# Sums of squares and decay sums in two rounded passes in a two-block transformer kernel

## What is computed

```
q = rms_norm(q, sb_q_norm_w); k = rms_norm(k, sb_k_norm_w)      # stick-breaking branch
z = q @ k.T * scale                                             # by blocks of 128 rows
log_1mb = where(causal, log_sigmoid(-z), 0)
suffix = cumsum(log_1mb, reverse) - log_1mb
a = where(causal, exp(log_sigmoid(z) + suffix), 0);  o_sb = a @ v
...
qkv = silu(causal_depthwise_conv(gdn_qkv, gdn_conv_w))          # gated delta rule branch
gq = l2_normalize(gq); gk = l2_normalize(gk)                    # x * rsqrt(sum(x*x) + eps)
g = -exp(a_log) * softplus(gdn_a + dt_bias)
gc = cumsum(g);  decay = exp(gc_i - gc_j) for j <= i
T = inverse(eye + strictly_lower(k_beta @ k.T * decay))         # per chunk
o_gdn = chunked recurrence over states with T, decay, exp(gc)
```

## Time and profile before

| | us |
|---|---|
| median of 3 runs | 2774.71 |
| runs | 2766.96 to 2775.35 |
| profiled execution | 2777.7 |
| its span | 2776.0 |
| TensorE busy in it | 2666.2 (96%) |
| DVE, ACT, POOL busy | 1846.9, 1200.8, 527.0 |
| TensorE in the chain that ended last | 82% of the span |
| mean granted TensorE clock | 0.985 of full speed |

### The profile page before, as it was taken

How to read it: one execution, slowest core, us unless ns; L and a number is a source line. 1 busy time by engine, 2 the same in 40 slices (tenths; PEclk the granted TensorE clock), 3 DMA queues, 4 the chain that set the end, 5 groups by cost and what they waited for, 6 DMA issues and landing times.

```text
span 2776.0 us, 36053 instructions
## 1 busy us (share of the span) xinstructions
PE 2666.2 (96%) x13669; PEld 2289.8 (82%) x13669; DVE 1846.9 (67%) x3462; ACT 1200.8 (43%) x1941; POOL 527.0 (19%) x410
## 2 busy tenths in 40 slices
PE   8999999999998999999998999999999999999997
PEld 6887888887777999998997888888888656788886
DVE  4445665655665788876985888888987494544434
ACT  5554445343223444447994333333332454423222
POOL 0111111010001778772000111111110033000000
PEclk9999999999999999999999999999999999999999
DMA  4112110005662587865668898898986211222220
GB/s 168 54 54 83 70 46 31 31 31 212 210 213 104 215 299 279 280 230 203 256 245 297 331 346 336 331 350 321 344 336 219 82 57 49 97 91 91 97 101 31
DMA packets 141212, 501.14 MB, mean 181 GB/s; under 512 B 13256, under 2 KB 66928, under 8 KB 111472
## 3 DMA queue, kind: packets, MB, share of 16 engines
q1 hardware_dynamic: 122608, 364.60, 36.9%
q0 software_dynamic: 18432, 134.23, 12.2%
HBM read 450.53 MB, written 48.25 MB: 180 GB/s over the span
## 4 chain that ended last, share of the span: by engine, by line
PE 82%; DVE 8%; ACT 4%; DMA 3%; issue 1%; POOL 1%; SPq 0%; ACTq 0%; DVEq 0%; POOLq 0%
PE bank L250 22%; PE bank L252 22%; PE bank L251 22%; PE bank L2175 2%; DVE xn L1552 2%; DMA w_raw<-in_w_in_dram 2%; PE bank L1130 2%; PE bank L1146 1%; PE bank L2658 1%; DVE whl L246 1%; PE bank L748 1%; ACT whl L240 1%; PE bank L1136 1%; PE bank L2765 1%; PE bank L2692 1%
## 5 line engine op out<-in xcount | busy, mean ns | idle before, releaser
L250 PE MATMUL bank<-HH,uhl 128*128 128x384 f32 x1024 | 346.4, 338 | 1.9 <-POOL uhl L1678 1.9
L252 PE MATMUL bank<-HH,uhl 128*128 128x384 f32 x1024 | 343.5, 335 | 0.0
L251 PE MATMUL bank<-HL,uhl 128*128 128x384 f32 x1024 | 343.3, 335 | 0.0
L250 PE MATMUL bank<-vhl,awhl 128*128 128x512 f32 x768 | 301.6, 393 | 10.7 <-DVE awhl L2392 9.7
L251 PE MATMUL bank<-vhl,awhl 128*128 128x512 f32 x768 | 301.2, 392 | 0.0
L252 PE MATMUL bank<-vhl,awhl 128*128 128x512 f32 x768 | 300.7, 392 | 0.0
L1734 POOL DMA_INDIRECT gs<-in_uv_dram,idx x128 | 153.1, 1196 | 771.3 <-DVE x L1759 489.0
L2332 ACT ACTIVATE vhl<-vraw 128x1024 fp32r<-128x1024 f32 x128 | 135.7, 1061 | 324.3 <-PE bank L252 274.9
L1678 POOL TENSOR_TENSOR uhl<-ur,uhl 128x1024 fp32r<-128x1024 f32 x69 | 168.1, 2448 | 321.4 <-ACT uhl L1672 321.2
L246 DVE TENSOR_TENSOR whl<-w_raw,whl 128x2048 fp32r<-128x2048 f32 x49 | 113.9, 2325 | 168.5 <-ACT whl L240 168.5
L250 PE MATMUL bank<-HH,whl 128*128 128x512 f32 x528 | 213.9, 405 | 4.6 <-DVE whl L246 4.1
(11 more groups left out here) (434 smaller groups left out, 6105.6 us busy)
## 6 DMA issues: line engine op xcount, KB each, us to landing
ur<-in_peer_u_dram SPq DMA_DIRECT2D x128, 512.0 KB
vraw<-in_peer_v_dram SPq DMA_DIRECT2D x128, 512.0 KB
w_raw<-in_w_in_dram SPq DMA_DIRECT2D x36, 1024.0 KB, 4.9
xn<-in_ada_rows_dram SPq DMA_DIRECT2D x48, 512.0 KB, 4.7
g_scratch<-stg SPq DMA_DIRECT2D x12, 2048.0 KB, 8.2
gti<-g_scratch SPq DMA_DIRECT2D x16, 1536.0 KB, 12.3
wf_raw<-in_f_w_in_dram SPq DMA_DIRECT2D x22, 1024.0 KB, 4.8
act_scratch<-ag SPq DMA_DIRECT2D x96, 192.0 KB
```

What stands on the lines that cost most here:

```text
L250: e.matmul(out, l[0], r[0], start=start, stop=False)
L251: e.matmul(out, l[0], r[1], start=False, stop=False)
L252: return e.matmul(out, l[1], r[0], start=False, stop=stop)
```

## The change

Four edits, all in the mixer of the first block.

1. The matmuls with ones over squares, in both branches, become two fp32r passes: over the squares rounded, and over the rest. In the stick-breaking branch ACT rounds (into `eg_r`) right after the square, DVE subtracts (into `DT_r`), and the root of the tile before now follows these on ACT instead of leading. The very first sum moves behind the third projection. In group 0 of the delta rule DVE does both steps, for all four tiles, after its last weight split of the stage. In groups 1 to 3 ACT rounds the query squares in step 11, DVE subtracts in steps 12 and 13; the key squares move from step 16 to 14 and from the tile `cin` to the tile X of the inverse, DVE rounds and subtracts in step 15, their sums and roots move from step 18 to 16 and their normalisation from 20 to 18, while that of the query tiles goes from 15 to 20.
2. The decay sums become two fp32r passes over the high and low part of g (`ggr`), which DVE splits once.
3. For pair 3, ACT makes the high part of the logarithms, in step 2 ahead of the decays, and DVE only the low part, in step 2 ahead of the convolution; before DVE did both in step 3.
4. The new tiles lie over the same memory as fp32 tiles that are free at that time.

```diff
--- before.py
+++ after.py
@@ -452,17 +452,29 @@
...
+    ggr = new.sb("ggr", [P, 2, NT, 8], F32R)
...
+    DT_r = [new.sb(f"DT_r{i}", [P, S], F32R) for i in range(2)]
+    PM_r = [new.sb(f"PM_r{i}", [P, S], F32R) for i in range(2)]
+    eg_r = new.sb("eg_r", [P, 2, S], F32R)
...
-    squares_of = lambda g: ([cin[i % 2][:, 3:] for i in range(4)] if g else
-                            [zs[i // 2][:, (i % 2) * S:(i % 2 + 1) * S] for i in range(4)])
+    half_z = lambda x, i: x[i // 2][:, (i % 2) * S:(i % 2 + 1) * S]
+    squares_of = lambda g: ([cin[i][:, 3:] for i in range(2)] + [flat(HB[f]["X"]) for f in range(2)] if g else
+                            [half_z(zs, i) for i in range(4)])
+    sq_high = lambda g: ([x[:, :] for x in DT_r + PM_r] if g else [half_z(Llo, i) for i in range(4)])
+    sq_low = lambda g: ([x[:, 3:] for x in cin_r] + [flat(HB[f]["X_r"]) for f in range(2)] if g else
+                        [half_z(zs_r, i) for i in range(4)])
@@ -483,8 +495,9 @@
...
-        e.wait_ge(*A.of("sq", g, i))
-        e.matmul(b[:, :], ones, squares_of(g)[i], start=True, stop=True).then_inc(*T.up("gn", g, i))
+        e.wait_ge(*V.of("sq_lo", g, i))
+        e.matmul(b[:, :], exact("ones"), sq_high(g)[i], start=True, stop=False)
+        e.matmul(b[:, :], exact("ones"), sq_low(g)[i], start=False, stop=True).then_inc(*T.up("gn", g, i))
...
     def act_gdn_proj(e, R, g, i):
@@ -499,7 +512,7 @@
...
             elif g:
-                e.wait_ge(*V.of("gq", g - 1, 2 + i))
+                e.wait_ge(*V.of("gq", g - 1, i))
@@ -516,9 +529,28 @@
...
+        elif i < 2:
+            e.wait_ge(*V.of("cv", g, 4 + i))
...
-            e.wait_ge(*(V.of("gq", g, i - 2) if i >= 2 else V.of("cv", g, 4 + i)))
+            e.wait_ge(*GH[0].of("xt", 2 * g - 4 + i, LV - 1))
...
+    def act_gdn_high(e, g, i):
+        T, A, V, G = GP
+        e.wait_ge(*GH[2].of("vT", 2 * g - 2 + i))
+        e.wait_ge(*A.of("sq", g, i))
+        e.activation(sq_high(g)[i], squares_of(g)[i], ACT.Copy).then_inc(*A.up("sq_hi", g, i))
...
+    def dve_gdn_high(e, g, i):
+        T, A, V, G = GP
+        e.wait_ge(*A.of("sq", g, i))
+        e.tensor_copy(sq_high(g)[i], squares_of(g)[i]).then_inc(*V.up("sq_hi", g, i))
...
+    def dve_gdn_sqlow(e, g, i):
+        T, A, V, G = GP
+        e.wait_ge(*(A if g and i < 2 else V).of("sq_hi", g, i))
+        e.tensor_tensor(sq_low(g)[i], squares_of(g)[i], r32(sq_high(g)[i]),
+                        ALU.subtract).then_inc(*V.up("sq_lo", g, i))
...
     def act_gdn_root(e, R, g, i):
@@ -571,9 +603,12 @@
...
+        if h < 2:
+            e.wait_ge(*SB[2].of("g_lo"))
...
-            i = e.matmul(b[:, blk(tb)], gg[:, tb, h:h + 1].broadcast_to([P, P]), const("triu"), start=True,
-                         stop=True)
+            for part in range(2):
+                i = e.matmul(b[:, blk(tb)], ggr[:, part, tb, h:h + 1].broadcast_to([P, P]), exact("triu"),
+                             start=part == 0, stop=part == 1)
...
     def act_decay(e, R, h):
@@ -640,8 +677,9 @@
...
-        e.wait_ge(*A.of("sq", pair, wi))
-        e.matmul(b[:, :], ones, scr[wi % 2], start=True, stop=True).then_inc(*T.up("nrm", pair, wi))
+        e.wait_ge(*V.of("sq_lo", pair, wi))
+        e.matmul(b[:, :], exact("ones"), eg_r[:, wi % 2, :], start=True, stop=False)
+        e.matmul(b[:, :], exact("ones"), DT_r[wi % 2][:, :], start=False, stop=True).then_inc(*T.up("nrm", pair, wi))
...
     def act_sb_norm(e, pair, wi):
@@ -673,6 +711,8 @@
...
+            if (pair, seg) == (0, 2):
+                pe_sb_norm(e, 0, 0)
@@ -695,8 +735,6 @@
         if seg in (0, 2, 4):
...
         if seg < 4:
-            if seg:
-                act_sb_norm(e, pair, seg - 1)
@@ -705,6 +743,10 @@
...
+            e.wait_ge(*A.of("sq", pair, seg))
+            e.activation(eg_r[:, seg % 2, :], scr[seg % 2], ACT.Copy).then_inc(*A.up("sq_hi", pair, seg))
+            if seg:
+                act_sb_norm(e, pair, seg - 1)
@@ -718,6 +760,10 @@
     def dve_sb_proj(e, pair, seg):
         if seg in (0, 2, 4):
...
+        if seg < 4:
+            e.wait_ge(*SB[1].of("sq_hi", pair, seg))
+            e.tensor_tensor(DT_r[seg % 2][:, :], scr[seg % 2], r32(eg_r[:, seg % 2, :]),
+                            ALU.subtract).then_inc(*SB[2].up("sq_lo", pair, seg))
@@ -798,7 +844,7 @@
...
-        if seg == 3:
+        if seg == 3 and pair < 3:
@@ -809,6 +855,16 @@
...
+    def act_sb_high(e, hh):
+        T, A, V, G = SB
+        e.wait_ge(*G.of("L", 3, hh, NT - 1))
+        e.activation(Lhi[hh][:, :], Ls[hh][:, :], ACT.Copy).then_inc(*A.up("hi", 3, hh))
...
+    def dve_sb_low(e, hh):
+        T, A, V, G = SB
+        e.wait_ge(*A.of("hi", 3, hh))
+        e.tensor_tensor(Llo[hh][:, :], Ls[hh][:, :], r32(Lhi[hh][:, :]), ALU.subtract).then_inc(*V.up("lo", 3, hh))
...
     def dve_sb_sum(e, pair, hh):
@@ -856,7 +912,7 @@
...
-            e.matmul(b[:, 0:32], const("triu"), flat(gg), start=True, stop=True).then_inc(*T.up("gc"))
+            e.matmul(b[:, 0:32], r32(exact("triu")), flat(gg), start=True, stop=True).then_inc(*T.up("gc"))
...
     def act_ba(e, seg):
@@ -907,6 +963,10 @@
...
+            e.wait_ge(*V.of("g"))
+            e.tensor_copy(ggr[:, 0, :, :], gg[:, :, :]).then_inc(*V.up("g_hi"))
+            e.wait_ge(*V.of("g_hi"))
+            e.tensor_tensor(ggr[:, 1, :, :], gg[:, :, :], r32(ggr[:, 0, :, :]), ALU.subtract).then_inc(*V.up("g_lo"))
         if seg == 5:
@@ -929,7 +989,6 @@
...
-        pe_sb_norm(e, 0, 0)
@@ -990,6 +1049,7 @@
...
                         if seg == 2:
+                            act_sb_high(e, h)
...
                         if seg == 3:
@@ -1004,7 +1064,7 @@
...
-        e.tensor_copy(cst_r[:, i:i + 2, :], cst[:, i:i + 2, :]).then_inc(*SB[2].up("exact"))
+        e.tensor_copy(cst_r[:, i:i + 3, :], cst[:, i:i + 3, :]).then_inc(*SB[2].up("exact"))
@@ -1020,12 +1080,18 @@
...
+                    if seg == 2:
+                        dve_sb_low(e, 0)
+                        dve_sb_low(e, 1)
...
                         if seg == 2:
...
                         if seg == 3:
...
+        for i in (2, 3, 0, 1):
+            dve_gdn_high(e, 0, i)
+            dve_gdn_sqlow(e, 0, i)
@@ -1069,8 +1135,12 @@
...
+        X_r = [new.sb(f"X_r{i}", [P, NT, P], F32R) for i in range(2)]
...
+        for i in range(2):
+            HB[i].update({"X": X[i], "X_r": X_r[i]})
@@ -1320,8 +1390,9 @@
...
-                    if g < 3 and seg in (14, 18):
-                        pe_gdn_ones(e, R3, g + 1, (2 if seg == 18 else 0) + f)
+                    if g < 3 and seg in (14, 16):
+                        pe_gdn_ones(e, R3, g + 1, seg - 14 + f)
+                for f in range(2):
@@ -1349,12 +1420,14 @@
                     if seg == 11:
...
+                            act_gdn_high(e, g + 1, i)
...
+                    if seg == 14:
+                        for i in (2, 3):
+                            act_gdn_square(e, g + 1, i)
...
-                        if seg in (14, 18):
-                            act_gdn_root(e, R3, g + 1, (2 if seg == 18 else 0) + f)
-                        if seg == 16:
-                            act_gdn_square(e, g + 1, 2 + f)
+                        if seg in (14, 16):
+                            act_gdn_root(e, R3, g + 1, seg - 14 + f)
                         if seg == 17:
...
                         if seg == 19:
@@ -1378,9 +1451,15 @@
...
                     if seg in STEP:
...
+                    if seg in (12, 13):
+                        dve_gdn_sqlow(e, g + 1, seg - 12)
...
-                        if seg in (15, 20):
-                            dve_gdn_normed(e, g + 1, (2 if seg == 20 else 0) + f)
+                        if seg == 15:
+                            dve_gdn_high(e, g + 1, 2 + f)
+                            dve_gdn_sqlow(e, g + 1, 2 + f)
+                        if seg in (18, 20):
+                            dve_gdn_normed(e, g + 1, (2 if seg == 18 else 0) + f)
+                    for f in range(2):
                         if seg == 18:
...
                         if seg == 22:

```

More of the change, by code:

```diff
@@ L454, in build @@
     gg = new.sb("gg", [P, NT, 8])
[L455 to L459 removed]
+    ggr = new.sb("ggr", [P, 2, NT, 8], F32R)
+    new.sb("after_ggr", [P, 64])
+    with ExitStack() as ph:
+        cin = [new.sb(f"cin{i}", [P, S + 3], scope=ph) for i in range(2)]
+    cin_r = [new.sb(f"cin_r{i}", [P, S + 3], F32R) for i in range(2)]
+    qkv = [[new.sb(f"gq{i}", [P, S]) for i in range(8)]]
+    with ExitStack() as ph:
+        DTs = [new.sb(f"DTs{i}", [P, NT, P], scope=ph) for i in range(2)]
+        PMs = [new.sb(f"PMs{i}", [P, NT, P], scope=ph) for i in range(2)]
+        eg2 = new.sb("eg2", [P, 2, NT, P], scope=ph)
+    DT_r = [new.sb(f"DT_r{i}", [P, S], F32R) for i in range(2)]
+    PM_r = [new.sb(f"PM_r{i}", [P, S], F32R) for i in range(2)]
+    eg_r = new.sb("eg_r", [P, 2, S], F32R)
     EGs = [eg2[:, i, :, :] for i in range(2)]
@@ L622, in build @@
```

(12 more changed lines are left out.)

4 lines of the change are left out of this document (removed).

## The result

| | before | after |
|---|---|---|
| median, us | 2773.40 | 2783.46 |
| runs, us | 2766.96 to 2775.35 (6) | 2780.39 to 2787.76 (6) |
| profiled execution, its span | 2777.7, 2776.0 | 2784.2, 2782.4 |

The changed kernel is 10 us slower, ratio 1.0044 (95% interval 1.0030 to 1.0059). It lies in the range of the forecast (2763 to 2787) and just inside the likeliest case's own (2770 to 2784), but on the side to which the prediction gave 17 in 100: slower by over 0.3%. The forecast was +2.2 us.

The account below looks back on a forecast made before the run. TensorE, busy 96% of the span, was taken to bound the kernel, with in-order queues feeding it. Stage terms summed to -0.6 us, plus 2.8 for clock falls, on the median 2774.7: 2777 us, range 2763 to 2787.

Parts of the forecast that it names:

- the clock: TensorE's clock falling behind new waits: two of them cost 1.4 us each, +2.8 us.
- Two passes for one matmul: Sums of squares over 512 columns: 0.86 us becomes 0.46, saving 0.40 us in each of 32, 12.8 if all kept.
- rival 3: Two fp32r passes with "ones" cost as much as the fp32 matmul: 2781 us; chance 0.03.
- Blocks of pairs 1 and 2: Stick-breaking blocks: waits of 0.6 and 2.1 us behind DVE's queue, +1.1 us per block, +2.2 for two.
- Pair 3: Last logarithms: the 5.1 us wait becomes 0.4, bank waits of 2.0 and 2.4 come; projection and output 3.6 us earlier.
- First squares: First delta rule sums: TensorE waits 3.1 us behind DVE's weight split, key products start 2.8 us later.
- Groups: Delta rule groups 1 to 3: new waits outweigh savings, +0.5 us per group, +1.5 in all.
- Start: Start to pair 0: first sum's 0.8 us wait goes, four sums save 1.6, third subtraction 0.5 late; net -1.9 us.
- In the block in which pair 0's heads run: Stick-breaking block with pair 0's heads: ACT has 5.5 us more per step, nothing is late, -1.6 us.
- Decays: Decay sums in two passes of 128 columns: 0.4 us saved per two heads, four times; bounds 0 to 0.9.
- rival 2: Each new wait drops the clock: ten falls of 1.4 us give +13, 2788 us; decides from seven; chance 0.14.
- Rival 1: ACT and DVE chains are not late, overlooked slack hides the new steps: -22.9 us, 2752; chance 0.2.

Follow-up runs that it names:

- the first squares' reordering: The changed kernel with group 0's four casts and subtractions ahead of DVE's last weight split: 2776.80 us, ratio 1.0019 to the kernel before.
- where it was run alone: The kernel before with only pair 3's logarithms split by ACT and the decay sums in two passes: 2771.39 us, ratio 0.9998.
- +3.1 alone: The kernel before with only group 0's four delta rule sums of squares in two passes: 2776.03 us, ratio 1.0014.
- the sums were run alone: The kernel before with only the stick-breaking sums of squares in two passes: 2775.64 us, ratio 1.0019.
- the groups run alone: The kernel before with only the sums of groups 1 to 3 in two passes and their moved steps: 2776.54 us, ratio 1.0022.
- the reorderings: The changed kernel with queue steps reordered in softplus pairs, pair 3, first squares and groups; all together 2762.58 us, ratio 0.9966 to the kernel before.
- the groups' second order: The changed kernel with DVE rounding query squares, decay subtractions first, normalised tiles at steps 19 and 21: 2779.08 us, ratio 1.0022 to the kernel before.
- the version without the groups' passes: The changed kernel reordered in softplus pairs, pair 3 and first squares, with groups 1 to 3 as in the kernel before: 2762.76 us, ratio 0.9962.

## Why the prediction fell short

The way of reading was right, and nearly every wait came where it was put. That the time fell inside the likeliest case's range, half a microsecond from its end, is luck in part: in the profiled mixer the sum without the clock was 5 to 6 us too low and the clock's share another 5, both the same way, of which the medians show 8. Point by point, forecast and measured:

- **Two passes for one matmul** save 0.4 us a sum: right. Passes start 0.23 apart with "ones" too (the rows of the first squares' reordering), so rival 3 is out.
- **Blocks of pairs 1 and 2**, +1.1 each: measured +1.2, waits 0.65 and 1.65 for 0.6 and 2.1.
- **Pair 3:** waits 2.0 and 2.4 forecast, 1.87 and 3.02 measured. -3.6 forecast, -2.8 where it was run alone, -1.2 in the changed kernel, in which the clock fell behind the second wait, where the prediction had expected full clock. Alone it fell behind the first, and the prefix sums at half pace only shortened the second wait (1.46).
- **First squares:** wait 3.1 forecast and measured; +2.8 to the key products forecast, +3.1 alone and +3.4 in the whole.
- **Groups:** waits 1.4 and 2.0 forecast, 1.45 and 1.74 measured; +0.5 each forecast, +1.0 where the clock held and the wait for a state came out, which the prediction had left out.
- **Start:** -1.9 forecast, -1.4 measured, -2.0 where the sums were run alone, -1.9 on average over all kernels.
- **The step that failed first** is "In the block in which pair 0's heads run ... nothing is late: -1.6". Measured +0.8 alone. The prediction followed the operands of the prefix sums and the norms, not the bank that the value projection takes; it had done just that in pair 3. 2.4 us.
- **Decays**, 0.4 saved four times: nothing is saved, 0.05 by the rows. It lay within the bounds given, and the value taken was the wrong end.
- **The term that was most mis-sized is the clock.** Two falls of 1.4 were forecast, +2.8. Of the 13.2 us in the mixer about 8 are clock: 1.5 at 95 us (the same block with the same wait of 1.70 takes 58.15 without the fall), 1.6 at 255 (the 51.42 against the 49.82), some 0.3 in the sums at 285 and 1.9 behind them (interval 98.30 against the 96.40 of the groups run alone), 0.6 each at 385 and 485, 1.4 at 600, which is no price of the change. At 385 and 485 the whole interval is 1.7 longer, but 1.0 of that is there without a fall as well: over five kernels, groups 1 and 2 with the wait of 1.74 take 98.2 to 98.4 where the clock fell and 97.6 to 97.7 where it held. The order of the queues alone makes about +5 where -0.6 was worked out. These shares are differences of stretches, good to some tenths.

So rival 2 (each new wait drops the clock) was nearer than the forecast: 2788 was its time and 2783.5 is measured. It had set seven falls as the point from which it decides; there were six, one of them at a wait that is in both kernels, and the sum that was too low did about as much to the time as the clock's excess. Its assumption that every wait counts was too strong: the waits of 1.65 in the blocks and of 1.45 for XT brought no fall of their own. The Trainium skill, "TensorE: Matmul & The Clock Gate", section "HAM oscillation — how this bites in real kernels", tells of a kernel whose matmuls, about 2 us at a time, are shorter than the waits for data between them, and which falls to the slower clock at every one of these waits. The trace agrees that a wait can bring the fall, but not that each does: the waits of 1.74 in groups 0 and 1 of the changed kernel brought it, the same wait in group 2 did not, and over five kernels the clock fell within 2 us behind it in 9 of 15 places.

Rival 1 (chains not late, 2752) was wrong for the kernel as it was changed, and the reorderings show that there is slack, in another order of the same work: 2762.6, about half of what rival 1 had.

## What to carry to other kernels

When a step is added to an in-order queue, list what stands behind it on that queue, and for each of these not only who reads its result but who takes the buffer that it frees; both projections that came late had waited for such a bank. Put the new step where the engine would otherwise stand still, and not as the head of a queue in which it waits for another engine: the same work in another order was worth 21 us here. And before moving work from one fp32 matmul to two cheap passes, check the width: at 512 columns it halves the time, at 128 nothing comes of it.

## What the runs showed of the hardware

- Whether the clock falls behind a given wait isn't fixed by the wait. One of 2.65 us for PMs stands at the same place in the last group of all fourteen kernels. The clock fell behind it in nine and held in five, the kernel before among these (the earlier trace rows are of other places). Two windows, of the kernel before and of the version without the groups' passes:

```profile
590.00:595.00 5.00, 5.00 (x45) 1.00 0.85 300
```

```profile
580.00:585.00 5.00, 5.00 (x34) 0.69 1.00 345
```

  The wait of 1.70 for the value projection's bank brought a fall in five kernels of six. What decides it beside the wait stays open; no run was made for it alone.
- Falls came behind waits shorter than the 1.87 us that the prediction had taken for the least: 1.70 and 1.74 us, and in group 0 of the groups' second order behind one of 1.43 (window below), which stands in groups 1 and 2 as well and brought none there.

```profile
385.00:390.00 5.00, 4.01 (x19) 0.66 0.02 3
```

- Half pace costs little while another engine sets the pace: in the first squares' sums, at half clock from about 287 us on, a sum every 1.06 us was DVE's pace (0.45 + 0.61 for cast and subtraction, start to start), and the stretch is 0.3 longer than with the first sum at full clock. In the groups half pace hid the wait of 0.84 for a state.
- Sixteen fp32r passes of 128 columns took 1.90 us and the sixteen fp32 records of the same work 1.95, where passes of 512 columns take half of the fp32 time. Each of the sixteen has its own weight load of 128 columns, and they start 0.12 us apart. The Trainium skill, "TensorE: Matmul & The Clock Gate", section "LDWEIGHTS (loading the stationary operand)", puts the time of such a load at the weights' columns divided by 1.2 GHz, which makes 0.107 us for 128. By that rule the loads set the pace of both forms here, and the trace agrees with it in size. The prefix sums of the changed kernel fit it too, with a load of 128 columns for every pass: passes of 256 columns start 0.12 apart as well, and once two of 128 stand only 0.06 apart, so a pass of that width doesn't itself need 0.12.

```profile
90.82 0.28 PE L794 MATMUL bank<-Lhi,cst_r 128*128 128x256 f32 x1
90.94 0.28 PE L794 MATMUL bank<-Llo,cst_r 128*128 128x256 f32 x1
91.06 0.22 PE L794 MATMUL bank<-Lhi,cst_r 128*128 128x128 f32 x1
91.12 0.27 PE L794 MATMUL bank<-Llo,cst_r 128*128 128x128 f32 x1
```

  No run changed the loads, so it is argued and not shown.
